# HGRN2 heads: VectorE makes the right side of each decay level one level earlier

## The reference

```python
proj = h @ w_in                      # q, f, i (values), g: 1024 columns each
q = silu(q); log_f = log(lb + (1 - lb) * sigmoid(f)); k = (1 - lb) * sigmoid(-f)
# per head (8 heads of 128), chunk by chunk, bc = cumsum(log_f):
decay = exp(where(mask, bc[t] - bc[s], NEG))
a = einsum('td,sd,tsd->ts', q, k, decay)
o = (q * exp(bc)) @ state + a @ v
# then head rmsnorm, times silu(g), and @ w_out
```

## Time and profile before

| | |
|---|---|
| runs | 1940.43, 1935.50, 1936.68 us; median 1936.68 |
| profiled execution | 1943.37 us, span 1941.5 us |
| TensorE matmuls | 1898.2 us busy (98% of the span) |
| VectorE, ScalarE, GpSimd | 917.0, 576.1, 729.8 us busy |
| mean granted TensorE clock | 0.993 |

### The profile page before, as it was taken

One profiled execution on the slowest core, in us unless ns is written; L12 is line 12 of the kernel. 1 busy time (PEld: TensorE's weight loads), 2 busy tenths in 40 slices (PEclk: granted clock), 3 DMA queues, 4 the chain that ended last, 5 costly groups with the idle time before them and its releaser, 6 DMA issues. The chain is left out here.

```text
span 1941.5 us, 36854 instructions
## 1 busy us (share of the span) xinstructions
PE 1898.2 (98%) x15078; PEld 1626.5 (84%) x15078; DVE 917.0 (47%) x1225; ACT 576.1 (30%) x1226; POOL 729.8 (38%) x625
## 2 busy tenths in 40 slices
PE   9999999999999999999999999999999999999997
PEld 8778744888887888888867888767999999999996
DVE  3898687667565444444336777765200000000023
ACT  1443213455522111110036657533121211111102
POOL 6755422555644434444527777652200000000011
PEclk9999999999999999999999999999999999999999
DMA  9213750322215666631212111102957568778893
GB/s 333 88 55 146 274 193 31 99 83 76 82 44 189 211 208 216 216 121 60 103 66 67 67 67 66 57 12 83 330 198 249 198 226 288 252 268 323 330 366 120
DMA packets 82824, 313.58 MB, mean 162 GB/s; under 512 B 10121, under 2 KB 10641, under 8 KB 82529
## 3 DMA queue, kind: packets, MB, share of 16 engines
q1 hardware_dynamic: 75952, 289.73, 42.3%
q0 software_dynamic: 4464, 14.35, 2.2%
q10 hardware_dynamic: 2241, 7.14, 1.0%
HBM read 301.43 MB, written 9.75 MB: 160 GB/s over the span
## 5 line engine op out<-in xcount | busy, mean ns | idle before, releaser
L261 PE MATMUL banks<-sb_act,sb_ring 128*64 128x112 f32 (+9 forms) x5088 | 624.9, 301 | 3.4 <-issue 2.3
L261 PEld LDWEIGHTS banks<-sb_act,sb_ring 128*128 128x128 f32 (+1 forms) x5088 | 594.3, 174 | 27.8 <-issue 8.0
L261 PE MATMUL banks<-sb_x_norm,sb_ring 128*128 128x256 f32 (+3 forms) x1616 | 332.6, 406 | 2.9 <-ACT sb_ring L468 2.0
L261 PEld LDWEIGHTS banks<-sb_x_norm,sb_ring 128*128 128x128 f32 (+1 forms) x1616 | 242.9, 171 | 67.1 <-issue 30.2
L3722 DVE TENSOR_TENSOR sb_act<-sb_work,banks 128x192 f32<-128x192 f32 (+7 forms) x88 | 27.1, 308 | 494.4 <-PE banks L261 475.7
L443 POOL TENSOR_TENSOR sb_ring<-sb_ring 128x512 f32<-128x512 f32 x146 | 206.6, 1415 | 101.1 <-PE banks L261 52.9
L261 PE MATMUL banks<-sb_work,sb_ring 128*64 128x256 f32 (+2 forms) x1124 | 231.7, 407 | 2.0 <-ACT sb_ring L468 1.8
L261 PEld LDWEIGHTS banks<-sb_work,sb_ring 128*128 128x128 f32 (+1 forms) x1124 | 155.3, 165 | 56.6 <-issue 33.5
L3253 POOL DMA_INDIRECT sb_work<-first_expert_rows,sb_table x8 | 7.5, 937 | 443.1 <-DMA first_expert_rows<-sb_x_norm 441.0
L3524 ACT ACTIVATE sb_work<-banks 128x192 f32<-128x192 f32 (+7 forms) x88 | 25.8, 294 | 300.0 <-PE banks L261 277.7
L499 POOL TENSOR_TENSOR sb_act<-sb_act,sb_ring 128x256 f32<-128x256 f32 x75 | 71.7, 956 | 67.0 <-ACT sb_act L468 59.5
(11 more groups left out here) (529 smaller groups left out, 2584.8 us busy)
## 6 DMA issues: line engine op xcount, KB each, us to landing
sb_ring<-in_w_moe_up SPq DMA_DIRECT2D x176, 512.0 KB
sb_ring<-in_w_moe_down SPq DMA_DIRECT2D x64, 704.0 KB
sb_act<-in_cond_w SPq DMA_DIRECT2D x84, 512.0 KB, 3.7
sb_ring<-in_w_ffn_up SPq DMA_DIRECT2D x44, 512.0 KB
sb_ring<-in_w_h_in SPq DMA_DIRECT2D x32, 512.0 KB
sb_ring<-in_w_in SPq DMA_DIRECT2D x28, 512.0 KB
sb_ring<-in_w_m_in SPq DMA_DIRECT2D x24, 512.0 KB
sb_ring<-in_w_ffn_down SPq DMA_DIRECT2D x16, 704.0 KB
```

Source lines behind the costliest of these rows:

```text
L261: last = m.nc.tensor.matmul(out[part], weights[:, part], act, start=start, stop=stop, skip_group_check=skip)
```

## The change

The first right side of head 0 is made ahead of the loop. In each head the right side of level 2 comes right after the take of the previous head's level 7, and in each round j from 2 to 7 the take of level j-1 comes first, then the right side of level j+1 (in round 7 that of level 1 of the next head), and then the pair additions and whatever else the round holds. The right side of level j+1 goes into the buffer that level j-1 has been read from. `times`, `take` and `add` themselves stay as they are, and so do the lists of all other engines.

```diff
             inputs(S4)
             sums(0)
             forget(1)
+            times(0, 1)
             for h in range(HEADS):
                 q, k = q_of(h), k_of(h)
-                times(h, 1)
                 if h == 0:
                     sums(1)
                 else:
                     take(h - 1, LEVELS - 1)
+                times(h, 2)
                 step(nc.vector.memset(atts[h % 2], 0.0))
                 take(h, 0)
                 finishes = 1 if h == HEADS - 1 else 3
                 for j in range(1, LEVELS):
                     if j > 1:
-                        times(h, j)
                         take(h, j - 1)
+                        if j < LEVELS - 1:
+                            times(h, j + 1)
+                        elif h + 1 < HEADS:
+                            times(h + 1, 1)
                         add(h, j - 1)
                     if 0 < h < HEADS - 1 and j == 3:
                         sums(h + 1)
```

## The result

The changed kernel is slower: 1945.70 us (median of 6 runs, 1943.39 to 1947.13) against 1938.02 us (6 runs, 1934.40 to 1940.43) for the kernel before, ratio 1.0044 with a 95% interval of 1.0035 to 1.0054, so 6.8 to 10.5 us. The forecast was 1939.0, 2.4 us over before, and the range ended at 1944.0: the direction was right, the size was not. Slower by over 0.3% had been given 0.11.

The account below looks back on a forecast made before the run. TensorE's matmuls, filling 98% of the span, were taken as the bound. 1.19 + 1.96 + 1.26 - 2.0 = plus 2.4 us on 1943.37 gave 1945.8; less 6.7 to the median, 1939.0 us, range 1930.5 to 1944.0.

Parts of the forecast that it names:

- Step 1: Heads 2 to 5, level 5: the four "issue" waits of TensorE go, minus 0.70 us each.
- Step 2, C21 and P6: Heads 1 to 5: C22 stalls beside GpSimd, C21 and P6 come 1.19 us late; plus 1.19 and 1.96 us.
- rival 1: No stalls, C22 gets through ahead of GpSimd: together minus 3.7 us, 1933; chance 0.2.
- Step 2, the edges: Edges end about 0.5 to 1.2 us later, mostly covered; taken at nothing, 1 us in the bounds.
- Head 0: Over 1 us of slack in the C21 to P6 chain, so the delay there costs nothing.
- Step 3: Pairs of two gates, into heads 3 and 5: C21 0.63 us late, twice, plus 1.26 us; lower bound nothing.
- Step 4: Heads 6 and 7: long waits go, one of 4 to 5 us comes; minus 2.0 us, bounds minus 5 and nothing.
- Rival 2: Heads 6 and 7: long waits vanish for good; minus 5.4 us, 1931.3; chance 0.15.
- Rival 3: Heads 1 to 5: P6 waits grow to about 1.4 us and the clock falls; plus 10.9 us, 1947.6; chance 0.1.

Follow-up runs that it names:

- diff_one_more: Changed kernel, but each GpSimd difference waits for one more right side (n - 3 instead of n - 4): 1939.70 us, ratio 1.0013.
- diff_after_c21: Changed kernel, but GpSimd's difference in round 4 also waits for pair addition C21: 1950.08 us, ratio 1.0070.
- before_again: The kernel before, unchanged, run once more for a second profile: 1936.99 us.
- heads_6_and_7: The change in heads 6 and 7 only, the old order in heads 0 to 5: 1937.17 us, ratio 1.0001.
- after_again: The changed kernel, unaltered, run once more for a second profile: 1945.86 us.
- adds_first: Changed kernel, but each round's pair additions stand ahead of the moved right side: 1947.65 us, ratio 1.0060.
- before_gates_last: Kernel before, with only the second half of the gates moved behind the copy of values in round 5: 1932.60 us, ratio 0.9979.
- adds_first_diff: Changed kernel with pair additions ahead of the moved right side and each GpSimd difference waiting for one more right side: 1938.26 us, ratio 1.0006.
- adds_gates_diff: Changed kernel with additions first, GpSimd differences held one right side more, second half of gates behind the copy of values: 1933.95 us, ratio 0.9982.

## Why the prediction was wrong

**Step 1 was right.** The four waits went, 2.79 us.

**Step 2, C21 and P6, was right to the hundredth.** 1.19 us late was forecast, 1.20 read; the split of 0.46 for the order and 0.73 for the stall is shown by diff_one_more (0.47 left) and diff_after_c21 (0.72 gone). The row of the same instruction in the same collision was the right one to take. The argument against rival 1 held as well: the difference that collides depends on TensorE's level 2, as the take does, and did not move.

**Step 2, the edges, is the step that failed.** "If it falls short a few tenths are paid per head", with 1 us in all at worst: it was 2.95 us, 1.03 in heads 2 and 4. The edges were put 0.5 to 1.2 us late, which is the delay of C21 carried on. The stretch grew by 1.95 us. Of that 0.73 is the order (12.94 less 12.21: one more product, 0.46, and a little of the collisions) and 1.22 goes when GpSimd is held. The sentence behind it is "SP's and GpSimd's lists are untouched". The list is untouched; its start times are not, since GpSimd waits at L2921 for a right side, and these became earlier. The prediction had the fact: rival 1 says that "GpSimd's list is also moved by earlier right sides", but as a reason for fewer stalls, and no step priced it. The cover that it named, 0.49 of TensorE's own delay and 0.9 between edges and cross products, was about right (1.20 less 0.67, and 1.06 from 1151.40 to 1152.46), and 1.95 less both is 0.36, close to the 0.45 that head 3 paid. Heads 2 and 4 paid 0.6 more; in head 2 the last edge product lay beside one of GpSimd's left sides (1119.53 for 0.72 us):

```profile
1119.49 0.84 DVE L3074 TENSOR_SCALAR sb_work<-sb_work 128x128 f32<-128x128 f32 x1
```

(the kernel after; 0.84 us against 0.28 in head 3).

**Head 0** was taken at nothing and has a wait of 0.41 us, for ScalarE (L2787) behind the later add. "Over 1 us of slack" had no row.

**Step 3** had the right mechanism and was half a size too large: 0.43 us a pair, not 0.63. It lies between the bounds, 0 and 0.63. The step leant on the row of P5's 0.19 us; that wait stayed, and the new one, 0.42 us, stands one product earlier, at P6 of level 1.

**Step 4 failed in size.** The wait of level 4 went, one before level 1 of head 7 came (3.00 us, 4 to 5 forecast), and g6 ran at full clock, as it can without the change (before_again). Three waits took the gain back: 1.22 us before g6 (the C21 of step 2 again, which the wait of level 4 had hidden), 1.04 at the cross products of head 6, and 1.91 at those of head 7. All are the same late VectorE list, which had been priced in heads 0 to 5 and not carried on here. The copy of values came 2.26 us late, not 1.4, and ScalarE, as forecast, won back its 0.6: head 7's first decays are 1.66 us late (1268.99 less 1250.35, against 1260.39 less 1243.41). heads_6_and_7 shows the step alone as 1.0001. That g7 kept its clock in the first profile, where the low one was forecast, was luck: in after_again and in heads_6_and_7 it fell.

**Rival 2** at its own price, minus 5.4 us, lies inside the 5.8 us that can't be told from no change, so it did not support the 0.15 for faster. **Rival 3** named the P6 waits rightly as the danger, and not their price: at 1.35 to 1.40 us the clock stayed. But no single point between 1.25 and 2.9 us decides: the last section has waits of 2.0 and of 2.9 us with both outcomes. In the kernel after, the stretch around the wait of head 3 (1151.81):

```profile
1150.00:1154.00 4.00, 2.63 (x56) 2.52 (x53) 3.83 (x6) 2.75 (x6) 3.77 (x4) 1.00 0.00 0
```

The last three figures are the granted clock, 1.00, and no DMA. VectorE (3.83 of 4 us) and GpSimd (3.77) are both full: their instructions lie side by side all through it. The chance of 0.11 for slower was too small because the cost of the edges stood as a bound of 1 us in all, while 3.4 us more than the forecast, 0.85 a head in four heads, was enough to reach 0.3%, and because step 4 carried a gain of 2.0 us that did not come.

**The rule and the row.** The prediction weighed the Trainium skill (GPSIMD Engine Reference, Specifications), by which GpSimd shares SBUF interfaces with VectorE, and found the takes beside GpSimd slower than the rule would have them (0.74 us against 0.44). That reading was wrong. In the kernel before every take of levels 1 and 2 lasts 0.73 to 0.75 us and every take of levels 3 to 7 lasts 0.43 to 0.46, and the latter lie beside GpSimd too: in head 3 of the kernel after, the take of level 4 (1156.42, 0.44 us) lies wholly inside a left side (1156.16 to 1156.97). The length goes with the level, and no take shows a stall. After, C22 agrees with the rule (0.43 us alone, 1.15 beside the difference), and so do the gates (L3006, 1.15) and the first edge product (1.52). Whether the rule covers the last one, L3074, with one tensor as its input, no run here shows. The larger mistake was to use the rule for one instruction and not for all that come into reach.

## What to carry to other kernels

When an engine makes a result earlier, list everyone who waits for it, on every engine, and ask what they will now run beside: a list that isn't edited can still move, and a late release may have been what kept two engines apart. Set the length of the whole stretch on the busy engine against the length of the bottleneck's own work between the same two points; delays in the middle of it matter only through that, and a wait shortened ahead of the bound gives nothing (adds_first, diff_after_c21). And if an urgent instruction stands behind one that nobody waits for, move the latter back: before_gates_last took away with one edit the four waits that the change was meant for in heads 2 to 5, and no kernel measured is clearly faster.

## What the runs showed of the hardware

- The pair addition C22, both inputs in SBUF, over 13 of its kind on VectorE, 1030 to 1300 us (total busy time, mean ns), first in the kernel before:

```profile
L499 DVE TENSOR_TENSOR sb_act<-sb_act,sb_ring 128x256 f32<-128x256 f32 x13 | 9.5, 730 | 0.4
```

in the kernel after:

```profile
L499 DVE TENSOR_TENSOR sb_act<-sb_act,sb_ring 128x256 f32<-128x256 f32 x13 | 15.4, 1181 | 0.4
```

and in diff_one_more:

```profile
L499 DVE TENSOR_TENSOR sb_act<-sb_act,sb_ring 128x256 f32<-128x256 f32 x13 | 10.4, 802 | 0.4
```

The instruction is the same, and the mean follows where it stands against GpSimd's. Started 0.1 us ahead of GpSimd's difference it takes 0.42 us, and started behind it 1.15, ending 0.28 us after GpSimd does (1144.61 against 1144.33). Values between occur where less of the GpSimd instruction is left: 0.60 us in head 2 of adds_first_diff, again ending 0.29 us after it (1103.69 against 1103.40).
- A VectorE product of a tile and a column stretched as well: L3074, 0.84 instead of 0.28 us, beside GpSimd's left side. The pair additions with an input in PSUM stayed at 0.42 us in every kernel.
- The clock after a wait of 2.9 to 3.0 us of TensorE in heads 6 and 7 is not fixed. Over all profiles it fell in 9 such places (blocks of 8.00 to 8.77 us, or a granted clock of 0.50 to 0.58) and stayed in 5, two of them in before_again at the places where it had fallen in before. After 1.90 us before level 1 of head 7 it stayed in three kernels. So 1.7 us a place, as the prediction took it, is one of two outcomes and not a price. Of eleven waits of 2.00 to 2.30 us it fell after two: the 2.00 us of adds_gates_diff, and the 2.01 us at the cross products of head 4 in diff_after_c21 (granted clock 0.57 from 1192 to 1196), while the same wait in heads 2, 3 and 5 of that kernel left it at 1.00.
- A fall of the clock over g7 costs these kernels less than its 0.9 to 1.7 us. In the five profiles with right sides made ahead in head 7 where g7 ran at full clock (7.07 us), the cross products of head 7 then waited 1.32 to 1.91 us for their edges and started 17.62 to 18.78 us after g7 did; in the five where it took 8.00 to 8.77 us no wait is listed there, and they started after 17.05 to 17.80 us. In the changed kernel the execution with the fall got there 1.7 us sooner: the last two edge products took 0.29 and 0.28 us in it, and 0.75 and 1.30 beside GpSimd in the other.

What stays open: whether the wait of ScalarE's chain before level 1 of head 7 (1.90 to 3.00 us) can be taken away. adds_gates_diff made the copy of values earlier and the wait stayed at 2.00; no kernel changed ScalarE's own list. Nor was before_gates_last tried with GpSimd's differences held.
